# One-hots of the second keys made by ScalarE, one step ahead, in a two-block kernel with expert retrieval

## What is computed

```python
def peer(h, w_query, sub_keys_1, sub_keys_2, expert_down, expert_up):
    q = (h @ w_query).reshape(T, 8, 2, 128)
    s1, s2 = (q[:, :, i] @ keys_i.T for i in (0, 1))       # 128 keys each, 8 heads
    v1, i1 = top_k(s1, 16);  v2, i2 = top_k(s2, 16)
    top_s, pos = top_k(v1[..., :, None] + v2[..., None, :], 16)
    idx = i1[pos // 16] * 128 + i2[pos % 16]               # one of 16384 experts
    gate = softmax(top_s)
    act = sum_d(expert_down[idx] * h)                      # 128 experts a token
    return sum_k(gate * gelu(act) * expert_up[idx])
```

## Time and profile before

| what | us |
|---|---|
| median of 3 runs | 4364.61 |
| lowest and highest run | 4358.22 and 4368.15 |
| the profiled execution | 4355.47 |
| its span in the profile | 4353.8 |

### The profile page before, as it was taken

How to read it: one execution, slowest core, us unless ns; L and a number is a source line. 1 busy time by engine, 2 the same in 40 slices (tenths; PEclk the granted TensorE clock), 3 DMA queues, 4 the chain that set the end, 5 groups by cost and what they waited for, 6 DMA issues and landing times. The chain is left out here.

```text
span 4353.8 us, 40350 instructions
## 1 busy us (share of the span) xinstructions
PE 3377.1 (78%) x13955; PEld 1724.5 (40%) x13955; DVE 2524.5 (58%) x4423; ACT 409.2 (9%) x780; POOL 1624.5 (37%) x1133
## 2 busy tenths in 40 slices
PE   8989867899888884345888889988788844458888
PEld 6433333444765551111222248447655511112222
DVE  3768775500158778977555421521587788875553
ACT  1101003400011010000000012210111000000000
POOL 0000000000025665577676600000256655767774
PEclk9999979999999896666899999989999966678999
DMA  6333312244348998788999963323489977889998
GB/s 207 120 110 117 120 62 79 97 147 139 119 171 331 375 378 298 268 315 301 370 380 396 382 211 109 135 77 116 183 340 372 382 271 255 306 292 377 389 365 336
DMA packets 329280, 1066.49 MB, mean 245 GB/s; under 512 B 95635, under 2 KB 104675, under 8 KB 232291
## 3 DMA queue, kind: packets, MB, share of 16 engines
q0 software_dynamic: 147456, 717.84, 43.6%
q1 hardware_dynamic: 146528, 335.05, 22.0%
q10 hardware_dynamic: 35120, 11.33, 1.1%
HBM read 1417.99 MB, written 2.10 MB: 326 GB/s over the span
## 5 line engine op out<-in xcount | busy, mean ns | idle before, releaser
L1901 DVE CUSTOM_DVE_ANT_0 sc<-big,hs 128x2048 f32<-128x2048 f32 x512 | 1173.9, 2293 | 618.4 <-DMA big<-in_peer_down,sc 309.5
L672 PE MATMUL bank<-wring,ht 128*128 128x512 f32 (+1 forms) x1792 | 798.3, 604 | 2.4 <-ACT ht L1164 1.7
L982 PE MATMUL bank<-big,sc 128*32 128x512 f32 x4096 | 662.5, 739 | 104.0 <-DVE sc L1920 49.8
L923 PE MATMUL bank<-wring 128*128 128x512 f32 x1024 | 538.5, 662 | 91.0 <-DMA wring<-in_dense_up 85.7
L604 POOL DMA_INDIRECT big<-in_peer_up,sc x256 | 407.1, 1590 | 333.4 <-PE bank L982 197.6
L604 POOL DMA_INDIRECT big<-in_peer_v,sc x256 | 409.6, 1600 | 326.4 <-PE bank L982 202.7
L906 PE MATMUL bank<-ht,wring 128*128 128x256 f32 x2048 | 513.4, 405 | 20.5 <-DMA wring<-in_dense_down 20.5
L672 PEld LDWEIGHTS bank<-wring,ht 128*128 128x128 f32 x1792 | 345.3, 196 | 425.3 <-issue 419.5
L604 POOL DMA_INDIRECT big<-in_peer_down,sc x256 | 401.2, 1567 | 265.8 <-issue 212.1
L906 PEld LDWEIGHTS bank<-ht,wring 128*128 128x128 f32 x2048 | 400.5, 202 | 202.6 <-issue 125.6
L604 POOL DMA_INDIRECT big<-in_peer_u,sc x256 | 383.2, 1497 | 257.0 <-DVE sc L1876 140.6
(11 more groups left out here) (368 smaller groups left out, 2600.6 us busy)
## 6 DMA issues: line engine op xcount, KB each, us to landing
wring<-in_w_in SPq DMA_DIRECT2D x84, 1024.0 KB, 5.4
wring<-in_dense_down SPq DMA_DIRECT2D x64, 1024.0 KB
wring<-in_dense_up SPq DMA_DIRECT2D x256, 256.0 KB
wring<-in_w_out SPq DMA_DIRECT2D x32, 1024.0 KB, 5.0
wring<-in_w_attn_o SPq DMA_DIRECT2D x16, 1024.0 KB, 5.0
wring<-in_peer_w_query SPq DMA_DIRECT2D x16, 1024.0 KB, 5.0
wring<-in_peer_w_q SPq DMA_DIRECT2D x16, 1024.0 KB, 5.0
wring<-in_glu_w_a SPq DMA_DIRECT2D x8, 1024.0 KB, 5.1
```

The costliest lines, as they stand in the source:

```text
L672: mm = pe.matmul(dense_bank[2 * pair + t][:, 0:w_cols], lhs[:, k, t * P:(t + 1) * P], wslot[:, b, kk * w_cols:(kk + 1) * w_cols], start=(k ...
L923: mm = pe.matmul(dense_out[t][:, :], dense_w[:, r, t * P:(t + 1) * P], sup[:, m % 2, r % 4, :], start=(r == 0), stop=(r == DENSE - 1))
L982: mm = pe.matmul(acc_bank[j][32 * q:32 * q + 32, :], w_blocks[:, u % 2, g, :], gslot[:, m % RING, q * 512:(q + 1) * 512], start=(u % PH == ...
L1901: v.tensor_tensor_reduce(dot_out, gslot[:, m % RING, :], h[:, u // PH, :], 1.0, 0.0, ALU.mult, ALU.add, sub(rAC)[:, i:i + 1]).then_inc(dot ...
```

## The change

ScalarE makes `hot_b`, and the gate moves from `hot_a` to it. For each of a batch's 8 tokens it writes the distance of the pick's second key to 0 to 127, abs(i2 - iota), with the key as a bias read from SBUF. Then, in place, relu(gate - gate x distance), with the gate as bias and its negative as scale, both read from SBUF. That is the gate where the distance is 0, and 0 elsewhere (gates aren't negative). It does so in the step ahead of TensorE's, after whatever it has in that step. VectorE keeps the comparison for `hot_a`, also one step ahead, and in `take_selections` it also writes the negated gates into a part of `tok_sel` that is used up by then. Both semaphores, `hot_ready` and `sel_ready`, now count two each time.

```diff
--- before.py
+++ after.py
@@ -947,11 +947,11 @@
             def dense_gates(layer, hb):
 
                 n, bank = layer * NT * GATE_N + hb, dense_out[hb // 2 % 2]
-                pe.wait_ge(hot_ready, n + 1)
+                pe.wait_ge(hot_ready, 2 * n + 2)
                 if hb == 0:
                     pe.wait_ge(dd_evac, (layer + 1) * (DENSE // 2))
                 if hb % GATE_N == 0:
-                    pe.wait_ge(sel_ready, layer * NT + hb // GATE_N + 1)
+                    pe.wait_ge(sel_ready, 2 * (layer * NT + hb // GATE_N + 1))
                 if hb % 2 == 0 and n >= 4:
                     pe.wait_ge(gate_copied, n // 2 - 1)
                 for j in range(GATE_T):
@@ -1347,6 +1347,23 @@
                 act.activation(dense_w[:, 2 * p:2 * p + 2, :].rearrange("p r n -> p (r n)"), dense_out[p % 2][:, :],
                                ACT.Gelu).then_inc(dd_evac, 1)
 
+            def second_one_hots(layer, hb):
+
+                n = layer * NT * GATE_N + hb
+                t, c = hb // GATE_N, hb % GATE_N * GATE_T
+                if hb % GATE_N == 0:
+                    act.wait_ge(sel_ready, 2 * (layer * NT + t + 1))
+                if n:
+                    act.wait_ge(hot_mm, n)
+                i2, gate, minus = ([row[:, c + i:c + i + 1] for i in range(GATE_T)]
+                                   for row in (selT[:, t, 1], selT[:, t, 2], tok_sel[:, t, 0]))
+                for i in range(GATE_T):
+                    ins = act.activation(hot_b[:, i, :], iota_t[:, 0:P], ACT.Abs, scale=-1.0, bias=i2[i])
+                st.link(ins)
+                for i in range(GATE_T):
+                    ins = act.activation(hot_b[:, i, :], hot_b[:, i, :], ACT.Relu, scale=minus[i], bias=gate[i])
+                ins.then_inc(hot_ready, 1)
+
             def copy_gates(layer, b):
 
                 n = layer * GRP + b
@@ -1373,6 +1390,8 @@
                             dense_gelu(layer, p)
                         if gate_batch_at(n) is not None and gate_batch_at(n) % 2:
                             copy_gates(layer, gate_batch_at(n) // 2)
+                        if gate_batch_at(n + 1) is not None:
+                            second_one_hots(layer, gate_batch_at(n + 1))
                     row_gelu(base + u, u % 2)
 
             peer_head(0, a["ffn_norm_g"][0], (a["peer_sub_keys_1"][0], a["peer_sub_keys_2"][0]), R_PQ, 8)
@@ -1945,21 +1964,18 @@
             def take_selections(layer, t):
 
                 v.wait_ge(sel_done, layer * NT + t + 1)
+                v.tensor_scalar(tok_sel[:, t, 0, :], gate_bank[:, 2 * P:3 * P], -1.0, None, ALU.mult).then_inc(sel_ready, 1)
                 v.tensor_copy(selT[:, t].rearrange("p a n -> p (a n)"), gate_bank[:, 0:3 * P]).then_inc(sel_ready, 1)
 
-            def one_hots(layer, hb):
+            def first_one_hots(layer, hb):
 
                 n = layer * NT * GATE_N + hb
                 t, c = hb // GATE_N, hb % GATE_N * GATE_T
-                i1, i2, gate = (selT[:, t, j, c:c + GATE_T].unsqueeze(2) for j in range(3))
-                v.wait_ge(sel_ready, layer * NT + t + 1)
                 if n:
                     v.wait_ge(hot_mm, n)
-                st.add(v.tensor_tensor(hot_a, i1.broadcast_to([P, GATE_T, DENSE]),
-                                       dense_keys.unsqueeze(1).broadcast_to([P, GATE_T, DENSE]), ALU.is_equal))
-                st.link(v.tensor_tensor(hot_b, i2.broadcast_to([P, GATE_T, P]),
-                                        iota_t[:, 0:P].unsqueeze(1).broadcast_to([P, GATE_T, P]), ALU.is_equal))
-                v.tensor_tensor(hot_a, hot_a, gate.broadcast_to([P, GATE_T, DENSE]), ALU.mult).then_inc(hot_ready, 1)
+                v.tensor_tensor(hot_a, selT[:, t, 0, c:c + GATE_T].unsqueeze(2).broadcast_to([P, GATE_T, DENSE]),
+                                dense_keys.unsqueeze(1).broadcast_to([P, GATE_T, DENSE]),
+                                ALU.is_equal).then_inc(hot_ready, 1)
 
             def take_gates(layer, b):
 
@@ -2008,8 +2024,8 @@
                         hb = gate_batch_at(n - 2)
                         if hb is not None and hb % (16 // GATE_T) == 16 // GATE_T - 1:
                             take_gates(layer, hb // (16 // GATE_T))
-                        if gate_batch_at(n) is not None:
-                            one_hots(layer, gate_batch_at(n))
+                        if gate_batch_at(n + 1) is not None:
+                            first_one_hots(layer, gate_batch_at(n + 1))
                         if u in (PH, UNITS) and k % 4 == 0 and k:
                             add_row_sums(layer, u // PH - 1, k // 4 - 1)
                         if u == PH + 1 and k == 0:
```

## The result

| | median us | runs | profiled execution's span |
|---|---|---|---|
| before | 4366.38 | 4358.22 to 4371.72 (4) | 4353.8 |
| changed | 4254.39 | 4251.05 to 4257.81 (4) | 4249.3 |

A forecast was written before the change was run, and what follows sets the result against it. The gate stretches' pace was taken as VectorE's work plus late gathers. 79 us gain less 1 for negated gates and 16 for ScalarE's queue gave 62 us: 4302 us by the median, forecast 4275 to 4325, whole range 4250 to 4368.

The forecast's parts named there:

- four gate stretches: Where one-hots are made, two per block: first steps 88 to 132, second 133 to 165; the change lies there alone.
- the saturated stage: From step 170 on, limited by the DMA (share 0.99); claimed to start earlier and last as long, 400.7 us.
- ScalarE's price: Gate stretches: 16 new ACTIVATEs a batch take 5.7 us, some 365 us in all, with no table load added.
- The loop: Gate stretches: TensorE's multiply, ScalarE's batch and handovers take 7.3 us a batch, under today's 12.7 and 9.4 us.
- the rival itself: Second gate stretches: ScalarE's batch becomes the pace; at 10.5 us a batch, 37 us slower, 4402 us; chance 0.10.
- VectorE's cut: Gate stretches: 1.65 us a batch leaves VectorE, 105 us in all; 79 us of it counted as gain.
- VectorE's whole cut can be taken: First gate stretches: the full 26.4 us each is gained, steps going from 5.09 to 4.50 us.
- The lead: Gate stretches: gathers were issued late because TensorE stood behind VectorE; no term of its own in the sum.
- Slots come back sooner: Gate stretches: rows issued earlier, VectorE's row waits shrink, steps of 4.1 and 4.05 us; about 4248 us; chance 0.13.
- The DMA floor: Second gate stretches: busy share times step, 4.05 us, limits a step, so half the cut is taken: 4.3 us.
- The places in ScalarE's queue: Ten places where new ACTIVATEs and ScalarE's old work delay each other; 1.6 us each, 16 us lost.
- The full price of 75 us: Rival: ten places in ScalarE's queue cost 7.5 us each, 75 against 78; 4362 us, no change; chance 0.10.

The follow-up runs named there:

- scalar_long: The changed kernel with ScalarE's distances made three times over, each pass linked; 4432.52 us, ratio 1.0173.
- cut_no_lead: The changed kernel with VectorE's comparison for hot_a put back into TensorE's own step, ScalarE still one step ahead; 4313.68 us, ratio 0.9890.
- gates_after_rows: The kernel before with two calls exchanged on TensorE, so each step uses the up row before multiplying the one-hots; 4306.42 us, ratio 0.9882.
- lead_only: The kernel before with VectorE's three one-hot instructions moved one step ahead of TensorE, nothing taken off VectorE; 4291.92 us, ratio 0.9841.
- first_two_ahead: The changed kernel with two buffers for hot_a, filled by VectorE two steps ahead of TensorE; 4254.98 us, ratio 0.9767.

## Why the prediction was right or wrong

**The direction and the stage: right.** The gain lies in the four gate stretches, and the saturated stage behind them kept its length. The time, 4254.39 us, is below the 4275 to 4325 of the forecast itself. It lies in the whole range only because that reached down to a rival, at 4250.

**ScalarE's price: right.** 5.7 us a batch forecast, 5.66 measured. The distance step has 388 ns and the rectified step, with a scale from SBUF too, 480. By the Trainium skill, page "ScalarE: Activation LUTs", "What ACT_TABLE_LOAD costs", each pointer operand adds some 93 ns, and the trace agrees: 480 - 388 = 92. ScalarE's busy time rose by 356 us (330 to 400 forecast). There were no new table loads, 28 on L1341 as before; the Abs that starts at 1712.28 follows a Gelu of 1712.16 with none between. By the Trainium skill, page "ScalarE: Activation LUTs", "Table sets: the hidden batching unit", relu and abs are in every set; the rows agree, now for Relu and for Abs after Gelu too.

**The loop: place and point right, its price too low.** The forecast used it as a rival; `scalar_long` ran into it at 11.8 us a batch, and lost 178 us to the changed kernel where 170 were expected. But the rival itself priced a batch of 10.5 us at 37 us slower than before, and a batch of 10.6 us was 74 slower. It let the first stretches keep their whole 53 us. They kept 11: 224.0 and 221.2 us, against 229.1 and 227.5 before.

**VectorE's cut: the size was wrong.** I took 26.4 us in each first stretch and 13.2 in each second, 79 in all, as if VectorE's work were the pace. Alone it is worth 45 us, and 51 when it is put back into the changed kernel. The step that failed is "VectorE's whole cut can be taken", said of the first stretch: `cut_no_lead` gains 12.8 us there in block 0 and not 26.4, and 11.3 us in the second, where 13.2 were assumed; in block 1 the two are 11.3 and 5.5. VectorE idled 26 and 29 us for rows in the two stretches, and these rows came late because of the ring: the same waits are 13.8 and 8.8 us in `gates_after_rows`, with VectorE's work as it was. Work taken off VectorE partly turned into more of such waiting: in the first stretch 38.0 us in `cut_no_lead` against 25.8 before, and 22.3 in the changed kernel against 11.9 in `lead_only`.

**The lead: left out of the sum, and the larger half.** The forecast saw it ("a gather that was issued late because TensorE stood behind VectorE") and then gave it no term of its own. It stood only in the rival "Slots come back sooner", at 4248 us with a chance of 0.13. The kernel came out at 4254, but not by that rival's terms: it had the first stretches at 4.1 us a step and VectorE's waits for rows shrinking, and measured are 4.42 and 4.31 us, with these waits unchanged in sum. Lead alone is 67 us, and TensorE's order alone gives 55. That the forecast was off by only 48 us is luck in part, since two errors went against each other: 79 for 45 and 0 for 67, beside a loss of 16 (below) for next to nothing.

**The DMA floor: wrong.** Busy share times step, 0.86 x 4.71 = 4.05 us, was taken as a floor for the second stretch and halved the gain there. The changed kernel itself stays above it in block 0 (4.19), and block 1's 3.94 is above its own product from before (0.84 x 4.57 = 3.84). But the products went down, to 0.93 x 4.19 = 3.90 and 0.93 x 3.94 = 3.66, so they are no floor. `first_two_ahead` ran block 0's second stretch below 4.05, at 130.6/33 = 3.96 us a step:

```profile
1877.70:2008.30 130.60, 71.07 (x556) 23.93 (x556) 99.36 (x107) 91.16 (x256) 110.00 (x65) 0.70 0.96 360
```

The floor by bytes and the saturated rate (3.77) was not contradicted.

**The places in ScalarE's queue: 16 us forecast, next to nothing measured.** VectorE's wait for the Gelu of the dots, summed over the kernel, was 16.4 us before and is 11.7 now. Taking away most of ScalarE's batch took away all of TensorE's waits for ScalarE in block 0's gate stretches, and gained 3.6 us there. The order of ScalarE's queue was not changed by itself in any kernel. The full price of 75 us was far off.

## What to carry to other kernels

When an engine in order waits in front of work that is ready, and that work frees slots of a ring, price the wait through the ring and not through the two engines of the wait: here it was more than half of the gain, and exchanging two calls on TensorE gave 55 us without touching the slow engine. Lead and less work are separate terms. Give each its own number, since one kernel with each alone costs little and they may well add up, as here. Moving work to an idle engine at over three times the price (5.66 us for 1.65) was a good trade here, since the engine that it left was short of time, and its loop (wait, work, hand back) stayed shorter than the time between batches.

## What was not expected of the hardware

A small linked memset on POOL, 0.22 us long, moves the next gather by 0.71 us; the rest lies in the gaps around it. And the DMA's busy time isn't fixed by the work: in block 0's second gate stretch some 47.9 MB took a share of 0.86 over 155.3 us before (134 us of it) and 0.93 over 138.4 us in the changed kernel (129 us).
